# Row factor in PSUM, another order on VectorE and halved GpSimd operations at the entry of the seven-product part of a decoder layer's feed-forward

## The reference, cut to what matters

```
x = x + 0.5 * swiglu_ffn(x, ffn1_norm, w_gate, w_up, w_down)     # D_FF = 2816
x = x + mixers(rms_norm(x)) @ w_out                              # delta rule, block attention, memory attention
x = x + 0.5 * swiglu_ffn(x, ffn2_norm, w_gate, w_up, w_down)

def swiglu_ffn(x, gain, w_gate, w_up, w_down):
    h = rms_norm(x, gain)        # x * rsqrt(mean(x*x) + eps) * gain
    return (silu(h @ w_gate) * (h @ w_up)) @ w_down
```

## Time and profile before

| | us |
|---|---|
| three runs | 1027.97, 1033.41, 1031.24; median 1031.24 |
| the profiled execution | 1024.68, its span 1022.9 |
| TensorE busy | 1001.1 (98%), granted clock 0.995 |
| VectorE busy | 727.6 (71%) |
| GpSimd busy | 498.2 (49%) |
| ScalarE busy | 442.9 (43%) |
| the chain that ended last | TensorE 84%, VectorE 9%, GpSimd 4% |

### The profile page before, as it was taken

One profiled execution on the slowest core, in us unless ns is written; L12 is line 12 of the kernel. 1 busy time (PEld: TensorE's weight loads), 2 busy tenths in 40 slices (PEclk: granted clock), 3 DMA queues, 4 the chain that ended last, 5 costly groups with the idle time before them and its releaser, 6 DMA issues.

```text
span 1022.9 us, 16443 instructions
## 1 busy us (share of the span) xinstructions
PE 1001.1 (98%) x6826; PEld 879.4 (86%) x6826; DVE 727.6 (71%) x1085; ACT 442.9 (43%) x645; POOL 498.2 (49%) x273
## 2 busy tenths in 40 slices
PE   9989989999999999999999999999998999999998
PEld 7868879999999988788877788888787999999997
DVE  5896877667686488962556883789688766768646
ACT  7542434333434353444356664543243434343431
POOL 0336586657666323533262201535468665776630
PEclk9999999999999999999999999999999999999999
DMA  8332133323233032231211001322303332313312
GB/s 323 125 124 83 42 124 125 124 83 103 68 120 124 21 145 83 87 119 42 83 61 66 3 3 42 112 94 84 124 1 124 124 125 83 120 64 106 125 39 85
DMA packets 15770, 95.32 MB, mean 93 GB/s; under 512 B 2000, under 2 KB 2128, under 8 KB 5456
## 3 DMA queue, kind: packets, MB, share of 16 engines
q1 hardware_dynamic: 15696, 94.27, 26.6%
HBM read 92.16 MB, written 2.10 MB: 92 GB/s over the span
## 4 chain that ended last, share of the span: by engine, by line
PE 84%; DVE 9%; POOL 4%; DMA 1%; ACT 1%; issue 1%; DVEq 0%; POOLq 0%
PE bank L1832 48%; PE bank L1960 28%; POOL wlo L488 3%; DVE xn_ffn L1221 1%; DMA raw<-fast_in 1%; PE bank L2008 1%; DVE gbuf L1201 1%; DVE x L1307 1%; DVE t_ffn_sum L1239 1%; POOL t_ffn_lo L498 1%; PE bank L2247 0%; DVE sums L1255 0%; DVE prob L1590 0%; DVE sums L1256 0%; PE bank L2251 0%
## 5 line engine op out<-in xcount | busy, mean ns | idle before, releaser
L472 POOL TENSOR_TENSOR wlo<-raw,whi 128x2048 fp32r<-128x2048 f32 x30 | 145.1, 4841 | 246.3 <-ACT whi L557 244.4
L1960 PE MATMUL bank<-t_ffn_hi,whi 128*128 128x256 f32 x896 | 253.7, 283 | 1.2 <-DVE bank L1278 1.2
L1960 PE MATMUL bank<-t_ffn_hi,wlo 128*128 128x256 f32 x896 | 253.6, 283 | 0.0
L1960 PE MATMUL bank<-t_ffn_lo,whi 128*128 128x256 f32 x896 | 253.6, 283 | 0.0
L488 POOL TENSOR_TENSOR wlo<-sums,whi 128x512 fp32r<-128x512 f32 x128 | 193.8, 1534 | 62.0 <-ACT whi L671 61.8
L488 POOL TENSOR_TENSOR wlo<-raw,whi 128x512 fp32r<-128x512 f32 x96 | 140.2, 1474 | 85.9 <-ACT whi L671 85.9
L1960 PEld LDWEIGHTS bank<-t_ffn_hi,whi 128*128 128x128 f32 x896 | 172.0, 192 | 2.2 <-DVE bank L1278 1.6
L1960 PEld LDWEIGHTS bank<-t_ffn_lo,whi 128*128 128x128 f32 x896 | 171.9, 192 | 0.6
L1960 PEld LDWEIGHTS bank<-t_ffn_hi,wlo 128*128 128x128 f32 x896 | 171.9, 192 | 0.0
L1832 PE MATMUL bank<-ahi,whi 128*128 128x512 f32 x432 | 171.3, 396 | 0.3 <-POOL wlo L472 0.3
L1832 PE MATMUL bank<-ahi,wlo 128*128 128x512 f32 x432 | 168.5, 390 | 0.0
(11 more groups left out here) (309 smaller groups left out, 1484.2 us busy)
## 6 DMA issues: line engine op xcount, KB each, us to landing
raw<-fast_in SPq DMA_DIRECT2D x32, 1024.0 KB, 4.9
raw<-stream SPq DMA_DIRECT2D x30, 1024.0 KB, 5.0
raw_down<-fast_in SPq DMA_DIRECT2D x18, 1024.0 KB, 4.9
raw<-stream SPq DMA_DIRECT2D x6, 512.0 KB, 7.3
x<-x_in SPq DMA_DIRECT2D x4, 512.0 KB, 6.8
out<-x SPq DMA_DIRECT2D x8, 256.0 KB, 2.0
raw<-stream SPq DMA_DIRECT2D x4, 256.0 KB, 6.0
memx<-mem_in SPq DMA_DIRECT2D x2, 512.0 KB, 10.7
```

The source lines that it names most:

```text
L472: nc.gpsimd.tensor_tensor(wlo[:, u % RING, :], raw[:, u % RAW, :], whi[:, u % RING, :].bitcast(F32), ALU.subtract).then_inc(w_lo, 1)
L1960: ins = E.matmul(psum[bank][:, HALF * h:HALF * (h + 1)], a, b[:, k, :], start=start and k == 0 and m == 0, stop=k == K2 - 1 and m == 2, sk ...
```

## The change

Five edits. (1) `hidden` of the first group and `normalize` take r from a PSUM bank instead of from rbc: bank 7 in layer f = 0, where it is already, bank 5 in f = 1, to which VectorE copies rbc first. (2) TensorE waits for all eight instructions of normalize before each of the down products of the second and third weight groups, so that it does not overwrite the bank. (3) In VectorE's list T_4 stands directly behind T_2, and the sums of the up weights of body 0 behind residual adds 0 and 1. (4) down_low of body 0 stands ahead of weight_sums(f, 1, 0). (5) GpSimd's low parts of units 4 to 9 and 26 to 33 are two instructions of 1024 columns each; the semaphore counts after the second.

```diff
+        R_BANKS = [7, 5]
@@ split (GpSimd)
-                nc.gpsimd.tensor_tensor(wlo[:, u % RING, :], raw[:, u % RAW, :],
-                                        whi[:, u % RING, :].bitcast(F32), ALU.subtract).then_inc(w_lo, 1)
+                parts = 2 if U_SECOND[0] <= u < U_IN or u >= U_FFN[1] else 1
+                for c0 in range(0, 2048, 2048 // parts):
+                    c1 = c0 + 2048 // parts
+                    ins = nc.gpsimd.tensor_tensor(wlo[:, u % RING, c0:c1], raw[:, u % RAW, c0:c1],
+                                                  whi[:, u % RING, c0:c1].bitcast(F32), ALU.subtract)
+                ins.then_inc(w_lo, 1)
@@ hidden (VectorE)
-                    V.tensor_tensor(gbuf[:, a, :], gbuf[:, a, :], rbc[:], ALU.mult).then_inc(silu_scaled, 1)
+                    r = psum[R_BANKS[f]] if unit == 0 else rbc
+                    V.tensor_tensor(gbuf[:, a, :], gbuf[:, a, :], r[:], ALU.mult).then_inc(silu_scaled, 1)
@@ normalize (VectorE)
-                    V.scalar_tensor_tensor(out=x_norm[f][:, k, :], in0=x[:, k, :], scalar=col(gain + k), in1=rbc[:],
-                                           op0=ALU.mult, op1=ALU.mult).then_inc(xn_ready, 1)
+                    V.scalar_tensor_tensor(out=x_norm[f][:, k, :], in0=x[:, k, :], scalar=col(gain + k),
+                                           in1=psum[R_BANKS[f]][:], op0=ALU.mult, op1=ALU.mult).then_inc(xn_ready, 1)
@@ ffn (VectorE)
+                else:
+                    link(V.tensor_copy(psum[R_BANKS[f]][:], rbc[:]))
                 hidden(f, 0)
...
                 t_total(f, T_2)
-                weight_sums(f, 0, 1)
+                t_total(f, T_4)
                 ffn_add(d0 + KD, 0)
                 ffn_add(d0 + KD, 1)
+                weight_sums(f, 0, 1)
                 ffn_add(d0 + KD, 2)
                 ffn_add(d0 + KD, 3)
-                t_total(f, T_4)
                 hidden(f, 2, low=False)
...
                     combine(f, i, 1)
+                    down_low(f, i)
                     if i == 0:
                         weight_sums(f, 1, 0)
-                    down_low(f, i)
                     fix(f, i, 0)
@@ ffn (TensorE)
                     pe.wait_ge(w_lo, v + 3)
                     pe.wait_ge(h_lo, n0 + 2 * n)
+                    pe.wait_ge(xn_ready, KD * (f + 1))
```

## The result

The changed kernel takes 1021.05 us (median of 4 runs, 1020.87 to 1021.41), the kernel before 1031.55 us (4 runs, 1027.97 to 1033.41): 0.9903 of it, 95% interval 0.9876 to 0.9930, 10.5 us faster. The forecast was 1022.4 and 8.8 us. The two profiled executions lie closer together: spans of 1019.1 and 1022.9, 3.8 apart. That difference is the first thing to explain, since all steps of the forecast were read from that one execution.

What follows compares the result with a forecast made beforehand. TensorE, busy 1001.1 of 1022.9 us, bounds the kernel; only its idle time and lower-clock time can be won. Savings 4.1 + 0.8 + 2.2 + 1.7 = 8.8 us, so 1031.24 - 8.8 = 1022.4; forecast 1018 to 1026, full range 1014 to 1029.

Steps and rivals of the forecast that it cites:

- rival (c): VectorE instructions with x from SBUF, per-partition gain and PSUM stay blocked; entries unchanged or 0.6 worse; 1028 us; chance 0.05.
- Entry, first layer: First layer's entry: down tile 4's 4.66 wait and 1.7 tail go, new costs come; 4.1 us saved.
- new tile-6 wait of 1.7: First layer's entry: add 2 ends at 76.1, down tile 6 is due at 74.4, so TensorE waits 1.7 us.
- the 0.7 that the prediction had named: First layer's entry, down tile 6: wait of 0.7 us instead of 1.7 if T_1 misses its turn.
- The 0.6 for the halved unit: First layer's entry: with GpSimd's operation halved, TensorE starts the second gate tile 0.6 us later, a loss once.
- Entry, second layer: Second layer's entry: L1201 pair held by one half each, add 2 done at 718.1 instead of 718.9; 0.8 us saved.
- Before the seven products: Stretch in each layer: old waits and tail go, 3.85 us of new waits come; 2.2 and 1.7 us saved.
- 3.56 + 1.9: Block 0's down product, first layer: wait for the down low parts and its lower-clock tail, both gone; 3.56 and 1.9 us.
- 1.4 + 1.75: Before the seven products, each layer: new waits at down tile 6 (1.4 us) and first combine (1.75 us, before 0.58).
- (a): Old waits go and nearly no new ones come: 16 to 17 us saved, 1014.5 us; chance 0.13.
- (b): Turns go worse before the seven products, only the entries pay: 4 to 5 us saved, 1026.8 us; chance 0.13.
- (d): Lower clock behind each of eight short waits, 1.7 to 1.9 us each: 5.6 slower, 1036.8 us; chance 0.05.

Runs made afterwards that it cites:

- e7: Changed kernel with VectorE fixed first at the first layer's end, and down_low of body 0 behind weight_sums(f, 1, 0) again; 1016.74 us.
- e6: Changed kernel with VectorE fixed first at the first layer's end, and T_4 and body 0's up-weight sums in their old places; 1021.58 us.
- e9: Changed kernel with VectorE fixed first at the first layer's end, and T_4, up sums and down_low of body 0 in old order; 1020.09 us.
- e8: Changed kernel with VectorE fixed first at the first layer's end, and GpSimd's low parts whole again, 2048 columns each; 1013.69 us.
- e5: Changed kernel with VectorE fixed first at the first layer's end, row factor from SBUF again in normalize and first hidden unit, halves kept; 1020.79 us.
- e3: Changed kernel with VectorE fixed ahead of GpSimd where both start together at the first layer's end; 1014.35 us.
- e4: Changed kernel with VectorE fixed first at the first layer's end, and the factor multiplied into the up product in PSUM for every group; 1009.77 us.
- e2: Kernel before, with VectorE made to wait for GpSimd's unit at the first layer's end; 1032.77 us.
- e1: Kernel before, with GpSimd made to wait for VectorE at the first layer's end; 1025.86 us.

## Why the prediction was right, and where it was not

**The path.** Right: TensorE's own waits were all there was, and the forecast steps moved 10.8 us where 8.8 were named. No instruction of L1221's successor is above 1 us (0.74 us in the mean over sixteen, 1.56 before), so rival (c) is out, and L1227 ends at 59.5, 1.5 later than forecast, 1.2 of it the later start.

**Entry, first layer: 4.1 forecast, 5.7 measured.** The step "new tile-6 wait of 1.7" failed. T_1 was issued at 60.60, just behind a new half, and lost its turn (2.96 us), so GpSimd was ahead by one half, and only one of the two L1207 was blocked (3.49 for the pair): 0.55 of wait, near the 0.7 that the prediction had named for this. The 0.6 for the halved unit at 43.76 did not come in this execution: the two halves took 5.84 where the whole took 5.36, but TensorE, 1.2 later from its start-up, arrived at 45.00, when they had just ended (44.95). In e7, with a shorter start-up, it waited.

**Entry, second layer: 0.8 forecast, 0.6 measured.** 2.34 became 1.75. The start of the unit was 709.68, not 710.5, and both halves were met as described (4.69 for the pair).

**Before the seven products: 2.2 and 1.7 forecast, 2.3 and 2.2 measured.** The waits came as named, 1.31 (1.4), 1.58 (1.75), 0.25 (0.7) in the first layer, 1.31, 1.59 and none in the second. The chain of waits after shows what stands in the place of the earlier trace rows: the first load of block 1 is no longer on it, the low parts now stand at its head and no longer release the down product, and the down product with its short wait takes 146.46 - 134.86 = 11.6 instead of 12.80:

```profile
127.58 2.28 DVE wlo L1272
129.86 2.24 DVE sums L1261
...
134.21 1.73 DVE sums L1261
...
139.25 0.42 DVE bank L1291
139.67 0.33 DVE bank L1292
140.00 0.60 DVE x L1313
140.60 0.14 issue
140.74 5.72 PE bank L1840 x24
```

The times are those of the prediction once the whole is moved by 4.6 us (4.5 by the starts of the matmuls, 1.2 - 5.7): block 1's first load forecast at 127, so 122.4, measured 122.59; add 0's end forecast at 145.2, so 140.6, measured 140.60. What was wrong is which edit earns it. The prediction credits the moved low parts with 3.56 + 1.9 per layer and books the token order as a cost (1.4 + 1.75). By e6, e7 and e9 the moved low parts earn nothing, and the token order, T_4 with the weight sums, earns 7.2 us. VectorE's chain up to add 0 sets when down tile 4 runs; it starts with block 1's load in e6 and, the load now being earlier, with the low parts in the changed kernel. Waits of TensorE ahead of that point cost nothing while the chain is the later one; they only shorten the wait at its end, and two short ones leave the clock up where one of 4.5 does not. Nothing in the prediction's way of adding (old waits gone, new waits come) could tell the two edits apart.

**Halving** was priced at a loss of 0.6 and turns gained. By e8 no gain shows, and in e5, with halves and without the PSUM operand, the first entry waits as long as before (4.67 against 4.66).

**Rivals.** (a), 1014.5, meets what the kernel does with the toss won (1014.35) by coincidence: against before with the toss won that is 11.5 us, not 16 to 17, and the new waits came. (b), worse turns: no. (d), the lower clock behind each short wait: refuted, clock 1.00 behind 1.31, 1.58 and 1.75; it fell behind 2.73 and more, and in one execution of three behind 2.33. So the prediction's ground against (d), the one wait of 2.34 at 1.00, was weaker than it looked. The Trainium skill, TensorE: Matmul & The Clock Gate, section A second HAM failure mode: psum-queue depth-cycling, warns of such pauses; at these lengths and distances the traces do not show it.

**What was not foreseen:** the toss. The forecast subtracted steps of an execution that had won it from a median that had not. That the time came out near is luck in this point: the changed kernel loses the toss too (5.7 us at that place). Why all four of its runs lose, where before won 15 of its 45 runs beside the experiments (4 of 19, 10 of 19, 1 of 7), stays open: both engines start there within 0.03 us in either kernel. Between the profiled executions of the changed kernel and of e3 lie 6.1 us (1020.88 and 1014.82), 5.7 at that place and 0.2 in the start-up; the medians' 6.7 is larger because e3's profiled execution was the slowest of its five.

## What to carry to other kernels

Where VectorE and GpSimd share a stretch, put one of a VectorE instruction's two tensor inputs in PSUM rather than cut GpSimd's work finer: that was 6.4 us here, one more such operand 4.6, halving nothing that shows. Find the chain that ends last before you price a wait, since a short wait ahead of a longer one isn't a cost, and read more than one timed run before you trust a profile: two instructions of the two engines that are issued together are worth a wait that fixes their order (6.9 us).

## What the runs showed of the hardware

- A VectorE instruction with one SBUF and one PSUM tensor took inside GpSimd operations what it took outside them: 0.68 us for 128x512, 0.73 to 0.74 with a per-partition factor too (the sixteen L1227 of the changed kernel). One that also writes PSUM does so as well (L1208 in e4, 0.69 in the mean of twelve).
- Who gets the shared access holds it for the whole instruction. At 0.08 us apart the earlier one had it (e7); at 0.03 us GpSimd's row starts first in both profiled executions and each engine got it once: two levels of time, 6.9 us apart, in one unchanged kernel.
- The granted clock stayed at 1.00 behind waits up to 1.75 us in these kernels and was under it behind those of 2.73, 3.85, 4.03, 4.47 and 4.50, for 1.6 to 3.1 us of loss each. Behind one of 2.33 or 2.34 it stayed up in two executions (before, e2) and fell in a third (e1, 0.61 over 721 to 725).
